# Attention masks in pairs, a projection group with a late last row, a reordered pooling and moved sums of squares

## What is computed

```python
# first kind, twice: retention (4 heads) + top-k attention "DSA" (4) + dilated attention (8)
mixed = concat([retention, dsa, dilated]); x = x + mixed @ w_out
h = rms_norm(x, mlp_norm_w); x = x + square(relu(h @ w_up)) @ w_down
...
# even: 8 heads of softmax(q k^T / 8 + c_t - c_s) v, and a trailing mean over 2, 4, 8, 16 frames
mean = (cg - lagged) / minimum(t1, w); pooled = mean - u[:, :, g]     # w = 2, 4, 8, 16
pool = (pooled @ pool_w) * pool_scale
m = concat([attn, pool]) @ w_out
# odd: conv and a linear recurrence. Both, around the mixer and around the MLP:
x = x + rmsnorm(m, g)          # needs the sum of m*m over the features
```

## Time and profile before

| what | value |
|---|---|
| median of 3 runs | 2418.17 us (2417.23 to 2418.5) |
| the profiled execution, its own time | 2416.57 us |
| its span, first to last instruction | 2414.8 us |
| outside the span | 1.8 us |
| mean granted TensorE clock | 0.997 |
| PE busy | 2371.4 us, 98% |
| DVE, ACT, POOL busy | 1034.8, 956.0, 1049.1 us |

### The profile page before, as it was taken

The page is one execution under the profiler, slowest core; times in us unless marked ns, Lnnn a source line. Parts: engine busy times, 40 slices in busy tenths (PEclk is TensorE's granted clock), DMA queues, the critical chain, the costliest instruction groups (busy, mean ns, idle before and its releaser), DMA issues. The chain is left out here.

```text
span 2414.8 us, 29460 instructions
## 1 busy us (share of the span) xinstructions
PE 2371.4 (98%) x11832; PEld 1900.5 (79%) x11832; DVE 1034.8 (43%) x1906; ACT 956.0 (40%) x1338; POOL 1049.1 (43%) x831
## 2 busy tenths in 40 slices
PE   8999999999999999999999999999999999999997
PEld 6777688888877767888888769888889779788887
DVE  4687531121348865221126445322225768322224
ACT  5345542232343455332235455422124485322223
POOL 4435244454444253444545453443444334444442
PEclk9999999999999999999999999999999999999999
DMA  5223122323222121323233212322332312322331
GB/s 167 76 62 106 36 96 96 105 88 105 83 93 88 53 97 53 105 88 105 89 104 101 87 36 71 105 84 90 105 98 95 105 53 88 105 90 85 105 105 53
DMA packets 139624, 214.40 MB, mean 89 GB/s; under 512 B 7776, under 2 KB 66272, under 8 KB 139232
## 3 DMA queue, kind: packets, MB, share of 16 engines
q1 hardware_dynamic: 139488, 212.51, 27.1%
HBM read 208.30 MB, written 2.10 MB: 87 GB/s over the span
## 5 line engine op out<-in xcount | busy, mean ns | idle before, releaser
L273 POOL TENSOR_TENSOR w_lo<-raw,w_hi 128x512 fp32r<-128x512 f32 (+1 forms) x776 | 992.3, 1313 | 1312.4 <-ACT w_hi L263 1312.1
L311 PE MATMUL ps<-h_hi,w_hi 128*128 128x512 f32 x1696 | 683.2, 403 | 11.3 <-POOL w_lo L273 11.1
L311 PE MATMUL ps<-h_hi,w_lo 128*128 128x512 f32 x1696 | 663.6, 391 | 0.0
L311 PE MATMUL ps<-h_lo,w_hi 128*128 128x512 f32 x1696 | 663.2, 391 | 0.0
L263 ACT ACTIVATE w_hi<-raw 128x2048 fp32r<-128x2048 f32 (+2 forms) x205 | 362.3, 1781 | 569.1 <-PE ps L311 443.8
L311 PE MATMUL ps<-hid_hi,w_hi 128*128 128x512 f32 x992 | 391.7, 395 | 4.7 <-DVE hid_lo L946 2.7
L311 PEld LDWEIGHTS ps<-h_hi,w_hi 128*128 128x128 f32 x1696 | 318.6, 188 | 92.7 <-issue 18.3
L311 PE MATMUL ps<-hid_hi,w_lo 128*128 128x512 f32 x992 | 387.2, 390 | 0.0
L311 PE MATMUL ps<-hid_lo,w_hi 128*128 128x512 f32 x992 | 387.0, 390 | 0.0
L311 PEld LDWEIGHTS ps<-h_lo,w_hi 128*128 128x128 f32 x1696 | 318.4, 188 | 70.1 <-issue 5.6
L311 PEld LDWEIGHTS ps<-h_hi,w_lo 128*128 128x128 f32 x1696 | 318.0, 187 | 70.5 <-issue 0.4
(11 more groups left out here) (302 smaller groups left out, 2800.8 us busy)
## 6 DMA issues: line engine op xcount, KB each, us to landing
raw<-in_w_up SPq DMA_DIRECT2D x32, 1024.0 KB, 5.3
raw<-in_w_down SPq DMA_DIRECT2D x32, 1024.0 KB, 5.0
raw<-in_ffn_w_gate SPq DMA_DIRECT2D x44, 512.0 KB, 4.0
raw<-in_ffn_w_up SPq DMA_DIRECT2D x44, 512.0 KB, 5.0
raw<-in_w_in SPq DMA_DIRECT2D x20, 1024.0 KB, 5.0
raw<-in_ffn_w_down SPq DMA_DIRECT2D x20, 1024.0 KB, 5.0
raw<-in_w_out SPq DMA_DIRECT2D x8, 1024.0 KB, 5.4
raw<-in_ev_w_in SPq DMA_DIRECT2D x8, 1024.0 KB, 5.3
```

Source lines behind the costliest of these rows:

```text
L273: pool.tensor_tensor(w_lo[slot.buf][:, k, 0:slot.width], raw[r][:, k, 0:slot.width], w_hi[slot.buf][:, k, 0:slot.width].bitcast(F32), ALU. ...
L311: mm = pe.matmul(o, lh, rh, start=first and q == 0, stop=last and q == 2, skip_group_check=True)
```

## The change

Four parts:

1. **Masks in pairs.** At even i DVE masks units i and i+1 one after the other and then negates both columns at once. There are 64 negations of 128x2 in place of 128 of 128x1.
2. **out_c late.** PE waits for `mix_lo` 5 and runs six tiles of out_c before it waits for `mix_lo` 6, in both first layers.
3. **Pooling.** Windows 16, 8, 4, 2 in this order, at PE steps 17, 19, 20, 22; out_a from step 24 with two tiles a step. Bank n of the pooling projection now holds group 3-n.
4. **Sums of squares.** In the boundary inside the odd layer `take(1, 3)` goes ahead of `low(0, 2)`, and `add_m(1, 2)` is behind the return of the last boundary. The odd layer's last boundary leaves two blocks to PE: `sq_total` sums the accumulator, block 2 and block 3 (six matmuls, recorded as twelve) where it summed the accumulator and block 3 (four, recorded as eight).

```diff
+POOL_ORDER = (3, 2, 1, 0)
...
         def sq_total(pe, nm):
-            if nm.last_apart:
-                pe.wait_ge(sems[nm.used], nm.used0 + nm.blocks - 2)
+            if nm.apart:
+                pe.wait_ge(sems[nm.used], nm.used0 + nm.blocks - 1 - nm.apart)
                 for i in range(2):
                     pe.matmul(ps[:, nm.bank, 0:S // 2], ones, two(nm.acc)[:, i, :], start=i == 0, stop=False)
-                pe.wait_ge(sems[nm.ready], nm.sq0 + nm.blocks)
-                to = nm.buf[(nm.blocks - 1) % 2]
-                for i in range(2):
-                    mm = pe.matmul(ps[:, nm.bank, 0:S // 2], ones, two(to)[:, i, :], start=False, stop=i == 1)
+                for k in range(nm.blocks - nm.apart, nm.blocks):
+                    pe.wait_ge(sems[nm.ready], nm.sq0 + k + 1)
+                    for i in range(2):
+                        mm = pe.matmul(ps[:, nm.bank, 0:S // 2], ones, two(nm.buf[k % 2])[:, i, :], start=False,
+                                       stop=k == nm.blocks - 1 and i == 1)
...
-                low(0, 2)
-                take(1, 3)
-                add_m(1, 2)
+                if self.split_first:
+                    low(0, 2)
+                    take(1, 3)
+                else:
+                    take(1, 3)
+                    low(0, 2)
                 if pre is None:
...
                     return
+                add_m(1, 2)
                 add_m(1, 3)
...
             def negate(self, dve, i):
-                dve.wait_ge(*at("s_masked", self.u0 + i + 1))
-                sg["nmax"].by(dve.tensor_scalar(sn[:, i:i + 1], sx[:, i:i + 1], -SCALE, None, ALU.mult))
+                dve.wait_ge(*at("s_masked", self.u0 + i + 2))
+                sg["nmax"].by(dve.tensor_scalar(sn[:, i:i + 2], sx[:, i:i + 2], -SCALE, None, ALU.mult), 2)
...
-                    if i < n:
+                    if i < n and i % 2 == 0:
                         self.mask(dve, i)
+                        self.mask(dve, i + 1)
                         self.negate(dve, i)
...
-            pl.n_out[1].last_apart = not even
+            pl.n_out[1].apart = 0 if even else 2
...
-                pe.wait_ge(*at("mix_lo", 6))
+                pe.wait_ge(*at("mix_lo", 5))
                 pe.wait_ge(*at("ret_lo", 2))
-                rest(tiles_of(pl.out_c, FEAT, hid_hi, hid_lo))
+                rest(group_tiles(pe, pl.out_c, FEAT, hid_hi, hid_lo, late=at("mix_lo", 6)))
...
-                PM = 20
-                out_a, out_b = Pace(16, 25, 7), Pace(16, 32, 7)
+                pool_steps = (17, 19, 20, 22)
+                out_a, out_b = Pace(16, 24, 8), Pace(16, 32, 7)
...
-                    for m, w in enumerate(POOL_W):
-                        pool.wait_ge(sems["bank_free"], BANKS + HALF * pl.pool + m + 1)
+                    for n, m in enumerate(POOL_ORDER):
+                        w = POOL_W[m]
+                        pool.wait_ge(sems["bank_free"], BANKS + HALF * pl.pool + n + 1)
```

More of the change, by code:

```diff
@@ L450, in __init__ @@
                 self.i = len(Norm.made)
-                self.last_apart = False
+                self.apart = 0
                 self.blocks, self.acc, self.bank, self.scale, self.hf, self.of = blocks, acc, bank, scale, hf, of
@@ L1782, in _ @@
                         sg["pool_in"].by(pool.tensor_tensor(u[:, 32:], ub[i][:, 32:], u[:, 32:], ALU.subtract))
-                        pool.wait_ge(*at("pool_in", m + 1))
+                        pool.wait_ge(*at("pool_in", n + 1))
                 stream_lo(pool, s_end + (4 if even else 0))
@@ L1817, in _ @@
                     rest(tiles_of(pl.val, TOK(512)))
-                    pool_tiles = tiles_of(pl.pool, FEAT)
+                    pool_tiles = tiles_of(pl.pool, [(n, m * P, P, None) for n, m in enumerate(POOL_ORDER)])
                     pool_pace.emit(-1, pool_tiles)
@@ L1830, in pooling @@
                         pool_pace.emit(i, pool_tiles)
-                        g = i - PM
-                        if 0 <= g < 4:
+                        if i in pool_steps:
+                            g = pool_steps.index(i)
                             pe.wait_ge(*at("pool_in", g + 1))
-                            sg["pool_mm"].by(pe.matmul(ps[:, 4 + g, :], pw[:, g, :], u4[:, g, 16:], start=True,
+                            m = POOL_ORDER[g]
+                            sg["pool_mm"].by(pe.matmul(ps[:, 4 + g, :], pw[:, m, :], u4[:, m, 16:], start=True,
                                                        stop=True))
@@ L1912, in pooling @@
                                 stream_hi(act, s0 + s + 1)
-                        g = i - PM
-                        if 0 <= g < 4:
+                        if i in pool_steps:
+                            g = pool_steps.index(i)
                             act.wait_ge(*at("pool_out", g + 1))
-                            sg["pool_hi"].by(act.activation(hid_hi[:, 4 + g, :], u4[:, g, 16:], ACT.Copy))
+                            m = POOL_ORDER[g]
+                            sg["pool_hi"].by(act.activation(hid_hi[:, 4 + m, :], u4[:, m, 16:], ACT.Copy))
                     fox.scalar(act, pooling)
@@ L2071, in pooling @@
                     def pooling(i):
[L2072 to L2076, removed]
-                            dve.wait_ge(*at("pool_hi", g))
-                            sg["pool_lo"].by(dve.tensor_tensor(hid_lo[:, 3 + g, :], u4[:, g - 1, 16:],
-                                                               hid_hi[:, 3 + g, :].bitcast(F32), ALU.subtract))
-                        if 0 <= g < 4:
+                        for n, m in enumerate(POOL_ORDER):
+                            if i == pool_pace.step_of(16 + 4 * (n + 1)) + 1:
+                                evac(dve, pl.pool, n, u4[:, m, 16:])
+                        if i - 1 in pool_steps:
+                            g = pool_steps.index(i - 1) + 1
+                            dve.wait_ge(*at("pool_hi", g))
+                            m = POOL_ORDER[g - 1]
+                            sg["pool_lo"].by(dve.tensor_tensor(hid_lo[:, 4 + m, :], u4[:, m, 16:],
+                                                               hid_hi[:, 4 + m, :].bitcast(F32), ALU.subtract))
+                        if i in pool_steps:
+                            g = pool_steps.index(i)
                             dve.wait_ge(*at("pool_mm", g + 1))
-                            col = V_PSC + g
-                            sg["pool_out"].by(dve.tensor_scalar(u4[:, g, 16:], ps[:, 4 + g, :], vec[:, col:col + 1],
+                            m = POOL_ORDER[g]
+                            col = V_PSC + m
+                            sg["pool_out"].by(dve.tensor_scalar(u4[:, m, 16:], ps[:, 4 + g, :], vec[:, col:col + 1],
                                                                 None, ALU.mult))
```

## The result

| | median, us | runs | profiled execution | span | mean granted clock |
|---|---|---|---|---|---|
| before | 2418.17 | 5 (2416.05 to 2418.84) | 2416.57 | 2414.8 | 0.997 |
| changed | 2428.32 | 5 (2427.83 to 2429.41) | 2428.32 | 2426.5 | 0.998 |

The ratio is 1.0044, with a 95% interval of 1.003 to 1.0059: the changed kernel is slower by 10.2 us, clear of noise. The forecast was 2417.4 in a range up to 2421; the time lies outside it.

What follows compares the result with a forecast made beforehand. PE, busy 2371.4 of 2414.8 us, was taken as the bound. Terms +6.3 - 3.0 - 0.85 - 3.0 - 0.6 + 0.3 = -0.85 put the median at 2417.4 us, range 2414 to 2421: no change.

Steps and rivals of the forecast that it cites:

- The order of the pairs: Attention passes: Exp of an even unit also waits for the odd mask; +6.3 us without the pooling stretch.
- The walk of the turns: Going through even units: Exp 0.35 to 0.62 us later, lost by PE at each turn without slack.
- the pooling stretch: PE's waits between 1414 and 1430, pooling change and pairs together: 4.45 us where they were 5.3, so -0.85 us.
- The form of the negation: DVE's negations: 64 fewer at 0.154 us save DVE some 5 to 10 us; no term for 128x2 being slower.
- The late row: out_c in two layers: PE's 1.36 us wait for the low part goes, -3.0 us.
- The pooling: Widest group first: PE's 2.57 us wait for POOL goes, but new waits for ACT leave -0.85 us, pairs included.
- The clock: Pooling stretch: the granted clock probably stays at 1.00 where it had fallen, giving back 3.0 us.
- rival 1: Clock falls all the same, once, between 1414 and 1434, costing 1.5 to 3: 2419 to 2420.5 us; chance 0.17.
- The sums of squares: Odd layer's inner boundary -0.6 us; last boundary, with twelve recorded matmuls instead of eight, +0.3 us.
- The slower rival: Clock falls in other stretches too, two or three at 3 us each: 2423.4 to 2426.4 us; chance 0.05.

Runs made afterwards that it cites:

- two_narrow: The changed kernel with each pair's two maxima negated by two 128x1 operations, both still behind both masks; 2418.92 us, ratio 1.0001 to before.
- masks_single: The changed kernel with masks in pairs undone, each mask followed by its own 128x1 negation; 2409.7 us, ratio 0.9965 to before.
- pool_only: The kernel before with only the pooling change (widest groups first, out_a from step 24); 2413.79 us, ratio 0.9985.
- wide_single: The kernel before, order untouched, with 123 of the 128 negations made 128x2; 2426.89 us, ratio 1.004.
- two_inputs: The kernel before, order untouched, each one-column negation done as a product of two SBUF columns; 2428.55 us, ratio 1.0045.
- pairs_only: The kernel before with only masks in pairs and one 128x2 negation per pair; 2434.62 us, ratio 1.0071.

## Why the prediction was wrong

It failed at the first sentence on part 1. "A negation takes 0.154 us; 64 fewer save DVE 64 x 0.08 to 0.15, some 5 to 10 us, on an engine that isn't the bound." It took the duration of one form, 128x1, for another, 128x2, of which it had no row, and gave it no bounds. It counted the new form as a saving on DVE and put its delay to Exp at nothing. Measured, the new form takes 0.335 us on the mean and up to 1.25, because it waits for a running POOL instruction, and this just where Exp, the pT copy and PE's turn wait for it in a row.

Step by step:
- **The order of the pairs.** The walk of the turns was right in kind: the new waits stand where it put them (0.6 us expected near 171.3 in layer 0, 0.59 at 173.95 in the changed kernel; 0.35 expected at the second turn, 1.11 there, with a negation that is 0.55 us longer). In size, two_narrow is 9.2 us over masks_single on the same chip, where part 1 and its share of the pooling stretch came to some 8 in the sum (-0.85 without the -3.0, -0.6 and +0.3 of the other parts, the clock's -3.0 and POOL's wait of 2.6): 1 us under. The clock fell for 3.4 us in two_narrow and not in masks_single, and this can be up to 1.7 of the 9.2 us (half of 3.4). With the narrow form the whole came to +0.6 us of before (two_narrow), against my forecast of -0.8.
- **The form of the negation.** Not in the sum. It is the distance from two_narrow to the changed kernel: ratios 1.0001 and 1.0044, 10 us. The error is 10.9 us (2428.3 for 2417.4), so this is nearly all of it.
- **The late row.** -3.0 us expected, -3.3 measured alone, and the wait gone in both layers.
- **The pooling.** POOL's wait is gone, as said. Alone the part gives 4.2 us. In the changed kernel the stretch has this instead (POOL, DVE, PE; then windows of 4 us):

```profile
1435.98 1.25 POOL L274 TENSOR_TENSOR w_lo<-raw,w_hi 128x512 fp32r<-128x512 f32 x1
...
1436.21 1.05 DVE L926 TENSOR_SCALAR stat<-stat 128x2 f32<-128x2 f32 x1
...
1438.59 0.52 PE L858 MATMUL ps<-tab,p 128*128 128x128 f32 x3 [2.46 <-ACT p L965]
```

```profile
1433.00:1437.00 4.00, 2.32 (x17) 1.00 (x13) 3.66 (x6) 1.58 (x5) 3.93 (x3) 1.00 0.00 0
1437.00:1441.00 4.00, 1.75 (x14) 1.50 (x15) 3.16 (x11) 3.26 (x9) 1.99 (x2) 0.87 0.09 19
1441.00:1445.00 4.00, 4.00 (x26) 3.03 (x25) 0.17 (x1) 1.11 (x5) 0.00 (x0) 0.70 0.64 247
```

A negation met POOL's instruction at 1436.21 and took 1.05 us, and the turn behind it waited 2.46 us, 0.9 of it by the negation's surplus. That is nearly as much as POOL's pooling had cost there before (2.57).
- **The clock.** I said it would stay at 1.00. It fell once, at 1439.9, inside the window with 1.75 us of work and behind one with 2.32, and stood at 0.50 for 3.4 us, where it had been 6.8. In two_narrow it was 3.4 us too, and in masks_single and pool_only it did not fall at all. So what rival 1, at 0.17, describes did happen in the changed kernel, for half as long as before, behind a stretch that the long negations had thinned out. "PE's busy time falls by about 3 us" was wrong (0.5).
- **The sums of squares.** In the inner boundary 0.9 us of waiting where it was 1.2, so -0.3 where the sum had -0.6 with the wait behind it; no run has this exchange alone. At the end the twelve matmuls run as walked:

```profile
2413.05 1.13 PE L479 MATMUL ps<-p_more,tab 128*128 128x256 f32 x4 [1.03 <-DVE acc L685]
2414.02 1.89 PE L483 MATMUL ps<-sq_both,tab 128*128 128x256 f32 x8
```

The wait ahead of them is 1.03 us where it was 1.72, and they end 2.86 us after they begin where eight took 1.97: +0.2, the +0.3 of the sum.
- **The rivals.** The slower rival put 2423.4 to 2426.4 on a clock that falls in more stretches, at 0.05. The result was slower than that, by another mechanism. None of my rivals asked whether the new instruction is as fast as the old ones.

The trace before could have told. Here are groups of DVE by line, with least, middle and longest duration in ns: the low part of a head pair (two SBUF inputs), the copy of the reciprocal sums into `rb` (one SBUF input), the reciprocal itself, and the one-column negation:

```profile
L946 DVE TENSOR_TENSOR hid_lo<-key,hid_hi x16: 679/683/1781, 168.9 to 1464.4; 128x512 fp32r<-128x512 f32 x16
```

```profile
L934 DVE COPY rb<-stat x16: 426/428/1295, 152.6 to 1452.7; 128x512 f32<-128x512 f32 x16
```

```profile
L931 DVE RECIPROCAL stat<-stat x16: 192/193/203, 152.4 to 1452.5; 128x8 f32<-128x8 f32 x16
```

```profile
L920 DVE TENSOR_SCALAR stat<-stat x128: 152/153/157, 129.7 to 1450.3; 128x1 f32<-128x1 f32 x128
```

The first has one form, 128x512, and durations from 679 to 1781 ns. The copy, with one input as the new negation has, goes from 426 to 1295: 5 of its 16 are long, and all 5 met a POOL instruction and ended 0.28 us behind its end. The reciprocal, also one input and several columns, stays at 192 to 203, and the one-column negation at 152 to 157. So the rows at hand allowed either answer for 128x2, and that was a reason for a range. The longest of the first group stands beside POOL like this:

```profile
213.13 1.29 POOL L1237 TENSOR_TENSOR retqk<-retqk,cos_t 128x512 f32<-128x512 f32 x1
...
213.19 1.78 DVE L946 TENSOR_TENSOR hid_lo<-key,hid_hi 128x512 fp32r<-128x512 f32 x1
```

POOL's instruction ends at 214.42; the DVE operation, which started just behind it in time, ends 0.55 us later, a little less than its own 0.68. The other three long ones of this group (0.82 to 0.84 us) also end 0.55 us behind a POOL instruction. The spread of one form's durations was the sign that some forms of DVE operation wait for POOL, and POOL is busy 43% of the span.

## What to carry to other kernels

An operation that a change adds is priced by a row of exactly its form (inputs, columns, memory), and where no row has it, its bounds are those of all the nearest operations with the same number of inputs, their longest duration included (here 0.19 us of the reciprocal to 1.30 of the copy). A group whose longest duration is far over its middle one waits for something: find out for what before putting more of its kind on a path that other engines wait for. On DVE, beside a busy POOL, a chain of small operations stays fast as one-column, one-input operations; merging two into one wider operation saved 64 instructions on an engine that was 43% busy and cost 10 us.

## What the runs showed of the hardware

- A DVE tensor_scalar from SBUF to SBUF of 128x2 in fp32 waits for the end of the POOL instruction that is running. One of 128x1 doesn't: in the kernel before none of 128 was over 157 ns, though 43 of them started while a POOL instruction had 0.1 us or more to run. A tensor_tensor of 128x1 with two SBUF inputs waits too (34 of 128 long, up to 1.24 us). A one-input copy of 128x512 waited (5 of 16), and a reciprocal of 128x8 didn't: the one at 1431.55 stood wholly inside a POOL instruction and took 192 ns.
- The wait lasts for what is left of POOL's instruction, here up to 1.25 us for an operation of 0.17, so its price goes by the length of POOL's instructions. There are exceptions. Behind POOL's scaling of the trailing mean (a tensor_scalar of 128x496) the wait ended 0.83 us before POOL's recorded end. And three negations of wide_single and two of two_inputs that started at the very end of one POOL instruction ended with the next.
- How often the clock fell differed between kernels with nearly the same PE work. In the pooling stretch it was not at all, for 3.4 us or for 6.8 us. It also fell for 3.4 us in each of the two DSA passes of pairs_only, and once near 871, in layer 1, in wide_single and two_inputs. Which idle pattern decides stays open; these runs were not made for it.
